# The last two tiles' products, the next tiles' splits and the residual's update, put in another order around each norm

## The reference

```python
def first_block(x, ...):
    for i in range(DEPTH):
        ...
        x = _layer_norm(DEEPNORM_ALPHA * x + mix, ln_gain[i, 0], ln_bias[i, 0])
        x = _layer_norm(DEEPNORM_ALPHA * x + swiglu_ffn(x, ffn_w_up[i], ffn_w_down[i]),
                        ln_gain[i, 1], ln_bias[i, 1])
    return x

def second_block(x, ...):
    for l in range(DEPTH):
        h = rms_norm(x, norm1_g[l])
        proj = h @ w_in[l]
        ...
        x = x + mixed @ w_out[l]
        h2 = rms_norm(x, norm2_g[l])
        x = x + peer(h2, peer_wq[l], peer_k1[l], peer_k2[l], peer_u[l], peer_v[l])
    return rms_norm(x, final_g)
```

## Time and profile before

| | us |
|---|---|
| median of 3 runs | 3069.22 |
| lowest, highest | 3065.42, 3070.78 |
| the profiled execution | 3074.24 |
| its span in the trace | 3072.4 |
| TensorE busy in it | 2896.7 (94%) |
| VectorE busy | 1956.4 (64%) |
| ScalarE busy | 1573.0 (51%) |
| mean DMA rate | 156 GB/s |

### The profile page before, as it was taken

How to read it: one execution, slowest core, us unless ns; L and a number is a source line. 1 busy time by engine, 2 the same in 40 slices (tenths; PEclk the granted TensorE clock), 3 DMA queues, 4 the chain that set the end, 5 groups by cost and what they waited for, 6 DMA issues and landing times.

```text
span 3072.4 us, 54820 instructions
## 1 busy us (share of the span) xinstructions
PE 2896.7 (94%) x19827; PEld 2656.8 (86%) x19827; DVE 1956.4 (64%) x3147; ACT 1573.0 (51%) x2874; POOL 23.2 (1%) x38
## 2 busy tenths in 40 slices
PE   8989998997899889999999999998899999999998
PEld 7978998996799779999999888877899999978886
DVE  4555554445445775996787555558499778855554
ACT  3434444445544554445776444455444477744444
POOL 0000000001000000000000000000000000000000
PEclk9989999998999999999999999999899999999999
DMA  6415555555355424454444555543345544455554
GB/s 210 158 62 170 187 185 155 182 174 94 110 185 184 134 83 147 163 164 158 139 144 131 184 191 190 190 157 110 117 159 163 167 141 138 144 171 191 190 189 141
DMA packets 131003, 480.14 MB, mean 156 GB/s; under 512 B 14608, under 2 KB 14608, under 8 KB 130480
## 3 DMA queue, kind: packets, MB, share of 16 engines
q1 hardware_dynamic: 126432, 460.38, 45.7%
q0 software_dynamic: 4432, 17.87, 2.4%
HBM read 477.02 MB, written 1.18 MB: 156 GB/s over the span
## 4 chain that ended last, share of the span: by engine, by line
PE 79%; DVE 14%; ACT 5%; issue 1%; DMA 1%; POOL 0%; DVEq 0%; ACTq 0%; SPq 0%; POOLq 0%
PE ps L1447 23%; PE ps L1449 23%; PE ps L1448 23%; DVE wl L779 5%; PE ps L1914 4%; ACT wh L362 2%; PE ps L1548 1%; PE ps L1694 1%; DVE mh L1317 1%; DVE picks L1319 1%; DVE arena L1141 1%; DVE mh L1311 1%; PE ps L1726 1%; PE ps L1880 0%; DMA raw<-stream_dram 0%
## 5 line engine op out<-in xcount | busy, mean ns | idle before, releaser
L779 DVE TENSOR_TENSOR wl<-raw,wh 128x1024 fp32r<-128x1024 f32 x878 | 1075.7, 1225 | 926.9 <-ACT wh L362 921.4
L362 ACT ACTIVATE wh<-raw 128x1024 fp32r<-128x1024 f32 x878 | 930.1, 1059 | 1294.9 <-PE ps L1449 1285.3
L1447 PE MATMUL ps<-xh,wh 128*128 128x256 f32 x4448 | 1291.4, 290 | 42.8 <-DVE wl L779 30.5
L1448 PE MATMUL ps<-xl,wh 128*128 128x256 f32 x4448 | 1262.1, 284 | 0.0
L1449 PE MATMUL ps<-xh,wl 128*128 128x256 f32 x4448 | 1261.3, 284 | 0.0
L1447 PEld LDWEIGHTS ps<-xh,wh 128*128 128x128 f32 x4448 | 856.2, 192 | 65.0 <-issue 38.6
L1448 PEld LDWEIGHTS ps<-xl,wh 128*128 128x128 f32 x4448 | 857.4, 193 | 0.3
L1449 PEld LDWEIGHTS ps<-xh,wl 128*128 128x128 f32 x4448 | 856.2, 192 | 0.0
L1447 PE MATMUL ps<-wh,mh 128*128 128x512 f32 x1264 | 503.4, 398 | 26.2 <-DVE ml L791 13.8
L1449 PE MATMUL ps<-wh,ml 128*128 128x512 f32 x1264 | 500.2, 396 | 0.0
L1448 PE MATMUL ps<-wl,mh 128*128 128x512 f32 x1264 | 499.0, 395 | 0.0
(11 more groups left out here) (275 smaller groups left out, 1870.6 us busy)
## 6 DMA issues: line engine op xcount, KB each, us to landing
raw<-stream_dram SPq DMA_DIRECT2D x878, 512.0 KB, 3.3
arena<-bias_scratch POOLq DMA_DIRECT2D x16, 384.0 KB, 6.6
arena<-norm_rows POOLq DMA_DIRECT2D x4, 1024.0 KB, 6.0
arena<-keys_dram POOLq DMA_DIRECT2D x2, 1024.0 KB, 5.2
arena<-ret_c_dram POOLq DMA_DIRECT2D x1, 1344.0 KB, 5.9
xr<-x_dram POOLq DMA_DIRECT2D x1, 1024.0 KB, 9.3
out_dram<-arena POOLq DMA_DIRECT2D x2, 512.0 KB, 2.9
arena<-rg_w_dram POOLq DMA_DIRECT2D x2, 256.0 KB, 3.0
```

The costliest lines, as they stand in the source:

```text
L362: A(wh[b % 2][:, :, :], raw[:, b % 4, :].rearrange("p (a b) -> p a b", a=DB), ACT.Copy) \
L779: V.tensor_tensor(wl[b % 2][:, :, :], raw[:, b % 4, :].rearrange("p (a b) -> p a b", a=DB), wh[b % 2][:, :, :].bitcast(F32), ALU.subtract) ...
L1447: M(out_ap, lh, rh, start=first, stop=False, skip_group_check=skip)
L1448: M(out_ap, lh, rl, start=False, stop=False, skip_group_check=skip)
```

## The change

Four edits, in the order of the diff:

- GpSimd's first load of the attention bias waits for the fourth chunk's update (`n_up`) rather than for a low part.
- ScalarE: in `mix_tiles` the high part of tile g + 8 stands ahead of the evacuation of tile g + 6, and a new one, of tile g + 9, ahead of that of tile g + 7. In `norm` the high part of tile nxt + 1 no longer stands behind the eight blocks: it follows the second chunk's root (in the mixer norms it is that of g + 9).
- VectorE: `lo(nxt + 1)` stands ahead of the eight blocks of `xl` in the rms and the mixer norms, and behind them in the others as before. In layer norms that are followed by tiles, `lo(nxt + 2)` and `lo(nxt + 3)` stand ahead of the first and the second chunk's update; the blocks that follow begin with later tiles. A wait of `updated` that an earlier step of the same stream fulfils is gone.
- TensorE: `last_pair` waits for the first of its tiles alone, and multiplies three of its four products (both halves of chunk 0, one of chunk 1) before it waits for the second.

```diff
@@ -316,7 +316,7 @@
             pool.wait_ge(b_vecc, G3)
             pool.dma_start(scratch.rearrange("g h x -> h g x"), bv[0:AH, :, :]).then_inc(b_store, 16)
             pool.wait_ge(b_store, 16)
-            pool.wait_ge(w_lo, START["att"] + 4)
+            pool.wait_ge(n_up, 4)
             for h in range(AH):
                 if h >= 4:
                     pool.wait_ge(a_b, h - 3)
@@ -410,7 +410,8 @@
                     if j < 6:
                         hi(g + j + 2)
                     evacuate(g + j, e + j, mixed[:, j % 4, :])
-                hi(g + 8)
+                    if j >= 6:
+                        hi(g + j + 2)
 
             def norm(k, nxt=None):
                 kind, source, gain, bias = NORMS[k]
@@ -428,8 +429,8 @@
                     link(A(squares, xr[:, c, :], ACT.Square, accum_out=nst[:, c, 2:3], **centre))
                     A(nst[:, c, 3:4], nst[:, c, 2:3], ACT.Sqrt, bias=vec[:, eps:eps + 1], scale=1.0 / D) \
                         .then_inc(n_std, 1)
-                    if nxt is not None and c == 0 and source != "mix":
-                        hi(nxt)
+                    if nxt is not None and source != "mix":
+                        hi(nxt + c)
                 if k in (3, 8):
                     return
                 for b in range(DB):
@@ -438,7 +439,6 @@
                         A(xh[:, b, :], zT[b], ACT.Identity, bias=vec[:, bias + b:bias + b + 1]).then_inc(n_hi, 1)
                     else:
                         A(xh[:, b, :], zT[b], ACT.Copy, scale=vec[:, gain + b:gain + b + 1]).then_inc(n_hi, 1)
-                hi(nxt + 1)
 
 
             act.wait_ge(const_in, 32)
@@ -849,7 +849,6 @@
 
                 def updated(c):
 
-                    dve.wait_ge(n_zc, 2 * ln_before[k] + c + 1)
                     V.scalar_tensor_tensor(out=xr[:, c, :], in0=zc[:, c, :], scalar=nst[:, c, 4:5],
                                            in1=ln_rows[:, 1, :], op0=ALU.mult, op1=ALU.add).then_inc(n_up, 1)
 
@@ -868,8 +867,8 @@
                                            in1=ln_rows[:, 0, :], op0=ALU.mult, op1=ALU.mult).then_inc(o_ready, 1)
                 if ln:
                     centred(1)
-                elif split and source != "mix":
-                    lo(nxt)
+                elif split:
+                    lo(nxt + 1 if source == "mix" else nxt)
                 scaled(1)
                 if k == 3:
                     updated(1)
@@ -878,8 +877,10 @@
                                            in1=ln_rows[:, 0, :], op0=ALU.mult, op1=ALU.mult).then_inc(o_ready, 1)
                 if not split:
                     return
-                if ln and source != "mix":
-                    lo(nxt)
+                if ln:
+                    lo(nxt + 1 if source == "mix" else nxt)
+                elif source != "mix":
+                    lo(nxt + 1)
                 for b in range(DB):
                     dve.wait_ge(n_hi, split_before[k] + b + 1)
                     if ln:
@@ -890,10 +891,12 @@
                         V.scalar_tensor_tensor(out=xl[:, b, :], in0=zT[b], scalar=vec[:, gain + b:gain + b + 1],
                                                in1=xh[:, b, :].bitcast(F32), op0=ALU.mult, op1=ALU.subtract) \
                             .then_inc(n_lo, 1)
-                lo(nxt + 1)
                 if ln:
-                    updated(0)
-                    updated(1)
+                    if source != "mix":
+                        lo(nxt + 1)
+                    for c in range(NC_T):
+                        lo(nxt + 2 + c)
+                        updated(c)
 
 
             dve.wait_ge(const_in, 32)
@@ -1012,7 +1015,7 @@
                 def rest(u, i=None):
                     pair_lo(fm[:, u % 2, :].rearrange("p (a t) -> p a t", a=2), u0 + u, i, 2)
 
-                for j in range(4):
+                for j in range(2, 4):
                     lo(g0 + j + 2)
                 mid(0, e0 + 4)
                 rest(0)
@@ -1031,7 +1034,9 @@
 
 
             g0, e0 = START["att"], EV["att"]
-            run(g0, 48)
+            lo(g0 + 4)
+            lo(g0 + 5)
+            run(g0 + 4, 44)
             values(g0 + 48, 16, 24, av)
 
             def softmax_max(n, s, st, views):
@@ -1483,18 +1488,19 @@
             def last_pair(b, u):
 
                 wait_tile(b, None, 0)
-                wait_tile(b + 1, None, 0)
                 pe.wait_ge(m_lo, u + 1)
-                for c in range(NC_T):
+                for j, c, h in ((0, 0, 0), (0, 0, 1), (0, 1, 0), (1, 0, 0), (1, 0, 1), (0, 1, 1), (1, 1, 0), (1, 1, 1)):
                     t = slice(c * P, (c + 1) * P)
-                    for j in range(2):
-                        s, w = 2 * (u % 2) + j, (b + j) % 2
-                        for h in range(2):
-                            ins = passes(ps_a[:, 2 * c + h, :], (mh[:, s, t], ml[:, s, t]),
-                                         (wh[w][:, 4 * h:4 * h + 4, :].rearrange("p a b -> p (a b)"),
-                                          wl[w][:, 4 * h:4 * h + 4, :].rearrange("p a b -> p (a b)")),
-                                         False, j == 1, skip=True)
-                    ins.then_inc(n_acc0 if c == 0 else mm_done, 1 if c == 0 else 2)
+                    s, w = 2 * (u % 2) + j, (b + j) % 2
+                    if (j, c, h) == (1, 0, 0):
+                        wait_tile(b + 1, None, 0)
+                    ins = passes(ps_a[:, 2 * c + h, :], (mh[:, s, t], ml[:, s, t]),
+                                 (wh[w][:, 4 * h:4 * h + 4, :].rearrange("p a b -> p (a b)"),
+                                  wl[w][:, 4 * h:4 * h + 4, :].rearrange("p a b -> p (a b)")),
+                                 False, j == 1, skip=True)
+                    if (j, c, h) == (1, 0, 1):
+                        ins.then_inc(n_acc0, 1)
+                ins.then_inc(mm_done, 2)
 
             def mix_turn(e, j):
```

## The result

| | before | the change |
|---|---|---|
| median, runs | 3070.0 us, 4 | 3042.05 us, 4 |
| lowest, highest | 3065.42, 3070.91 | 3040.74, 3045.93 |
| profiled execution, its span | 3074.24, 3072.4 | 3040.92, 3039.1 |

The ratio is 0.9926, 95% interval 0.9911 to 0.9941: 22.7 us faster (18 to 27). The forecast was 18.5 us and 3050.7 us, with 3045 to 3060 as its range. The way and the main mechanism held. The size was too small: 18.5 us lies at the low end of the interval, and the median lies 3 us under the range. By the ratio on the 3069.22 us of the time before it would be 3046.5.

What follows compares the result with a forecast made beforehand. TensorE streaming weights, 79% of the chain of waits, was taken as the bound. Terms 15.4 + 1.9 + 1.2 + 1.55 − 1.5 = 18.5 us, off 3069.2, gave 3050.7 us; range 3045 to 3060.

Steps and rivals of the forecast that it cites:

- Part 1: Last pair of tiles ahead of five norms: nine products go before the second tile's low part; 15.4 us gained.
- Parts 2 and 3: Tiles behind norms: earlier high part cuts second tiles' waits, 1.9 us; splits ahead of updates cut third tiles' waits, 1.2 us.
- Part 4: Mixers' last tiles: last evacuation 0.97 us later, yet first row 0.67 us earlier; 1.55 us gained over three mixers.
- rival of a table load with a tail: Mixers' Squares: a cost beyond the load's row comes out and takes back 1.55 us; 3052 us, chance 0.04.
- The turns: TensorE's 32 records at each norm: a longer wait ahead of them may slow them; a loss of 1.5 us taken.
- rival of the clock: Last pair: the clock falls all the same, 6.4 us less gain; 3057 us, chance 0.19.
- slower rival: Half clock moves onto dense products, two stretches at each of eight norms costing 25.6 us; 3076 us, chance 0.03.
- rival that hardly a difference is left: Clock, turns and waits for updates take most back, leaving 5 us of gain; 3064 us, chance 0.09.
- rival of first products that have to wait: Last pair: the first nine products would have to wait as well; no size or chance of its own.

Runs made afterwards that it cites:

- e1: The kernel before, with only the change's new order of the last pair's products; ratio 0.9947, median 3051.93 us.
- e3: The kernel before, with nine thrown-away products in TensorE's wait ahead of the last pair, old pair order; ratio 0.9975, median 3059.37 us.
- e10: The changed kernel, with the low part of the second next tile behind the eight blocks again in two rms norms; one run, 3041.41 us.
- e7: The changed kernel, with both updates ahead of the third tile's low part, as before; one run, 3048.28 us.
- e6: The changed kernel, with the root's table loaded ahead of the mixers' last evacuation and g + 9's splits behind the second root; ratio 0.9915, median 3039.0 us.
- e11: The changed kernel timed and profiled once more, unchanged; ratio 0.9925, median 3042.01 us.
- e4: The kernel before, profiled once more, unchanged; the stretches around the norms took 379.4 us.
- e5: The changed kernel, with thrown-away products in TensorE's wait ahead of each norm's turns; ratio 0.9905, median 3035.33 us.
- e2: The changed kernel, with the old order of products in the last pair; ratio 0.9986, median 3061.88 us.

## Why the prediction was right, and where its sizes were off

- **Part 1** was right by mechanism and size in four of the five norms: the first chunk comes 2.74, 2.97 and 2.79 us earlier in the first, second and seventh norm (2.83, 3.03, 2.86 said), the fourth norm's second chunk 3.00 (3.05), the last norm's 3.66 (3.73). e1 shows it alone, e3 splits it as the prediction did (1.46 clock, 1.37 products). In the seventh norm, between the two last layers, the first chunk does not decide: the first reciprocal stands on VectorE behind the second chunk's row, which waits for the pair's end. So the turns come 3.7 us earlier there, where 3.1 was said. The loss to the new low part behind the experts is there too, 0.6 us where 0.3 was said: the gain shrinks from 3.67 us at the turns of the second chunk to 3.06 at the last turn, and e10 shows the cause.
- **Parts 2 and 3** were mis-sized. From the last product's start of the first tile to the first of the second I find 0.84, 0.53, 0.50, 0.79, 0.49, 0.79 and 0.67 us before, and 0.40, 0.13 and five times 0.12 after: 3.5 us, where the sum had 1.9 (without the seventh norm). The idle column counts from a matmul's modelled end, 0.28 us behind its start, while the next may start 0.12 us behind it. So each such wait in the view is some 0.16 us short of what it costs. The third tiles give 1.4 us (1.2 said), and e7 confirms 1.1 of it.
- **Part 4** rested on a misreading. It put the two high parts ahead of the evacuations of g + 6 and g + 7, and so do the list in the section on the change and its last sentence; the diff, and the rows of its order, put each behind, and the high part of g + 9 stands between the last evacuation and the table load. The 0.97 us charged to the last evacuation does not exist: the row comes 1.66 us earlier instead of 0.67. ScalarE's high part and table load then decide, and the reciprocal comes 1.14, 0.55 and 0.55 us earlier, 2.2 us instead of 1.55. e6 shows that they decide: with both out of the way it comes 0.51, 1.10 and 1.10 us earlier still.
- The rival of a table load with a tail falls: in the change the Square stands right behind the load, 797.49 + 1.28 and a tiny activation, at 798.89, now without a wait that could hide a tail. Of the drain of 1.38 us that the Trainium skill, "ScalarE: Activation LUTs", section "What ACT_TABLE_LOAD costs", adds, nothing shows. The measurement decides.
- **The turns** were the term with the least ground. −1.5 us was said, and they took 2.7 us less in the first profile and 1.9 in e11, most of it in the first norm (5.25 to 3.96 us from first to last start, both times). But this is not shown to be the change's: e7 and e10, which have the change's order up to the turns of every norm, took 41.2 and 39.4 us in sum, as much as the kernel before or more (39.4, and 38.6 in e4), and 5.6 and 5.5 us in the first norm. Neither a gain nor a loss is shown. e5 shows that the wait in front of them is what they suffer from; which of them the half clock meets differs from execution to execution, and why, I leave open.
- The rival of the clock falls: granted 1.00 in the pair. The slower rival too: the mean granted clock of the execution rose from 0.974 to 0.980. The rival that hardly a difference is left falls by the interval of 18 to 27 us, and the rival of first products that have to wait falls as well: the first chunk stands 2.97 to 2.99 us behind the second low part's start in all five norms.
- The sizes together: the pair 16.0 us at the first turns of four norms and at the last norm's end (2.74 + 2.97 + 3.00 + 3.67 + 3.66), second tiles 3.5, third tiles 1.4, mixers 2.2, and the turns 2.7, which hold the 0.6 us lost in the seventh norm: about 26 us, against 26.3 in the norms' stretches and 22.7 (18 to 27) by the ratio. Of the 7.3 us that this is above the forecast, the turns are 4.2, part 2 is 1.6, part 4 is 0.7, part 1 is 0.6 and part 3 is 0.2. The largest of them is the one that isn't shown to be the change's, so how far the result lies from the forecast is in part luck. No run takes GpSimd's edit by itself.

## What to carry to other kernels

Where a last pair of operands ends a phase, multiply what the first one allows before waiting for the second, and put first what the next engine asks for. Price an idle TensorE by what may happen to the clock afterwards as well: here the clock was half of what the pair gained (7.7 of 16.3 us), and products with thrown-away results in the wait bought it alone. Take an order from the built program's rows, not from a reading of the diff, and a TensorE wait from the starts of its products.

## What the runs showed of the hardware

- A wait of 2.5 us on TensorE was followed by the half clock, 1.2 GHz, at 14 of 15 pairs in the three profiles with the old wait (nine of ten in the kernel before, five of five in e2), and by 2.4 GHz throughout at one (e4). With the wait filled by thrown-away products, the 12 products started 0.23 to 0.24 us apart on average in all five pairs (e3).
- 32 turns of fp32 data took 4.24 us at full clock and up to 6.77 us at half, not double. That they go at the pace of other engines' blocks at full clock is my reading, and no run tests it.
- The stretches between the norms took between 2674.4 and 2685.0 us in thirteen profiles. A gain below 5 us can be read from the places in the trace, and hardly from five timed runs.
